# A sixth weight slot for the experts of a two-layer hybrid trunk, with the residual's place lent to it

## What is computed

```
for i in range(2):
    h = rms_norm(x) * (1 + sc1) + sh1
    x = x + g1 * mixer_i(h)                      # gdn_mixer, then fox_mixer
    h = rms_norm(x) * (1 + sc2) + sh2
    # 32 experts of (1024 x 512) gate-up and (256 x 1024) down weights, 2 of them for each token
    x = x + g2 * sum_k w_k * (silu(h @ gate_e) * (h @ up_e)) @ down_e
return rms_norm(x, final_norm)
```

## Time and profile before

| | |
|---|---|
| Three timed runs | 1463.05, 1465.35, 1469.11 us; median 1465.35 us |
| The profiled execution | 1467.78 us, of which the span of instructions is 1466.2 us |
| TensorE busy in the span | 1337.1 us (91%) |
| VectorE, ScalarE, GpSimd busy | 731.8, 435.3, 397.0 us |
| Mean granted TensorE clock | 0.96 of full speed |
| DMA | 350.27 MB, mean 239 GB/s |
| Expert stages, first gather issued to last down product | 537.3 to 789.1 us and 1182.6 to 1437.2 us |

### The profile page before, as it was taken

How to read it: one execution, slowest core, us unless ns; L and a number is a source line. 1 busy time by engine, 2 the same in 40 slices (tenths; PEclk the granted TensorE clock), 3 DMA queues, 4 the chain that set the end, 5 groups by cost and what they waited for, 6 DMA issues and landing times.

```text
span 1466.2 us, 24949 instructions
## 1 busy us (share of the span) xinstructions
PE 1337.1 (91%) x9111; PEld 859.8 (59%) x9111; DVE 731.8 (50%) x1520; ACT 435.3 (30%) x1033; POOL 397.0 (27%) x588
## 2 busy tenths in 40 slices
PE   4999999999999989999886999999999979999881
PEld 2677767777775455555442777777764545555440
DVE  3656566667652466522223445666654557322224
ACT  4434424434442110000002645555541200000002
POOL 3022022112230023444334054434410024344320
PEclk8899999999999989999898899999999999999996
DMA  8255554512154279999997222122046379999995
GB/s 360 115 208 201 215 213 177 197 59 115 58 222 131 114 263 405 418 418 419 421 420 319 90 88 73 73 80 108 26 191 239 154 277 415 421 419 418 419 398 200
DMA packets 56693, 350.27 MB, mean 239 GB/s; under 512 B 18408, under 2 KB 18880, under 8 KB 30992
## 3 DMA queue, kind: packets, MB, share of 16 engines
q1 hardware_dynamic: 44992, 332.02, 57.1%
q0 software_dynamic: 11520, 16.83, 3.1%
q10 hardware_dynamic: 80, 0.04, 0.0%
HBM read 342.45 MB, written 27.34 MB: 252 GB/s over the span
## 4 chain that ended last, share of the span: by engine, by line
PE 70%; DMA 15%; DVE 9%; issue 2%; ACT 2%; POOL 1%; SPq 0%; POOLq 0%; DVEq 0%; ACTq 0%
PE PS L1116 10%; PE PS L771 8%; DMA hT<-in_moe_w_down_dram 8%; PE PS L773 7%; PE PS L772 7%; PE PS L1059 6%; PE PS L1123 5%; DMA Dr<-in_ada_w_dram 4%; PE PS L749 2%; PE PS L1143 2%; PE PS L1133 2%; PE PS L862 2%; PE PS L908 2%; PE PS L1108 2%; PE PS L1294 2%
## 5 line engine op out<-in xcount | busy, mean ns | idle before, releaser
L771 PE MATMUL PS<-hHi,Whi 128*128 128x512 f32 x512 | 225.3, 440 | 2.5 <-DVE hLo L1789 2.4
L773 PE MATMUL PS<-hHi,Wlo 128*128 128x512 f32 x512 | 202.8, 396 | 0.0
L772 PE MATMUL PS<-hLo,Whi 128*128 128x512 f32 x512 | 202.0, 394 | 0.0
L1360 ACT COPY arena<-PS 128x512 f32<-128x512 f32 (+4 forms) x256 | 108.6, 440 | 281.9 <-PE PS L862 104.7
L1116 PE MATMUL PS<-Wr,arena 128*64 128x256 f32 x1408 | 165.4, 389 | 9.8 <-DVE arena L2195 9.8
L1583 ACT ACTIVATE arena<-PS 128x128 f32<-128x128 f32 x72 | 20.0, 278 | 464.9 <-PE PS L1116 369.0
L1116 PEld LDWEIGHTS PS<-Wr,arena 128*64 128x64 f32 x1408 | 101.5, 140 | 88.8 <-issue 29.0
L2477 POOL DMA_INDIRECT y_rows<-arena x72 | 77.0, 1070 | 258.5 <-DVE arena L2207 252.2
L2418 POOL TENSOR_TENSOR Wlo<-Wr,Whi (+1 forms) x72 | 94.0, 1324 | 178.7 <-ACT Whi L1360 178.7
L771 PEld LDWEIGHTS PS<-hHi,Whi 128*128 128x128 f32 x512 | 97.6, 191 | 33.8 <-issue 18.2
L2201 DVE TENSOR_TENSOR arena<-arena,PS 128x128 f32<-128x128 f32 x72 | 20.7, 288 | 185.6 <-ACT arena L1583 169.0
(11 more groups left out here) (394 smaller groups left out, 2301.6 us busy)
## 6 DMA issues: line engine op xcount, KB each, us to landing
Wr<-in_moe_w_gate_up_dram SPq DMA_DIRECT2D x52, 2048.0 KB
Dr<-in_ada_w_dram SPq DMA_DIRECT2D x42, 1024.0 KB, 26.8
Dr<-in_moe_w_down_dram SPq DMA_DIRECT2D x28, 1024.0 KB
arena<-in_moe_w_gate_up_dram SPq DMA_DIRECT2D x14, 2048.0 KB
hT<-in_moe_w_down_dram SPq DMA_DIRECT2D x26, 1024.0 KB
Wr<-in_gdn_w_dram SPq DMA_DIRECT2D x8, 2048.0 KB, 8.6
Wr<-in_fox_w_dram SPq DMA_DIRECT2D x8, 2048.0 KB, 8.1
shift_scale<-in_moe_w_down_dram SPq DMA_DIRECT2D x12, 1024.0 KB
```

The source lines that it names most:

```text
L771: mm(out_ap, a_hi, b_hi, start=(k == 0), stop=False)
L772: mm(out_ap, a_hi, b_lo, start=False, stop=False)
L773: return mm(out_ap, a_lo, b_hi, start=False, stop=(k == KD - 1))
L1360: return nc.scalar.copy(dst, src)
```

## The change

- `FIRST` and `SLOTS` go from 5 to 6. The plan keeps 36 items and 33 places; expert 5 becomes one with an item of its own, and one ranked item fewer is planned at the end.
- The sixth down slot is a new tensor `spare` of 2048 columns, in which the first mixer's masks and sums now lie. It is asked for early (`down_load(i, 5, 5)`, right behind the down loads of slots 0 and 1). `busy` multiplies by `before` in place of `negmask`.
- The sixth gate-up slot is `X`. The residual is stored to `x_rows` (2048 KB) when the first two gathers have landed, the sixth gate-up matrix is asked for when that store has landed, and the residual is read back (2048 KB) when the last item that uses the slot has its gate-up product. `combine` waits for that.
- The down loads of slots 2, 3 and 4 are asked for behind that store, and so after the first two gathers have landed, in place of at `r_ps`.

```diff
-FIRST = 5
-SLOTS = 5
+FIRST = 6
+SLOTS = 6
...
-        if n < g - 1:
+        if n < g - 2:
             rank_at.append(one)
...
+        spare = sb("spare", [P, 2048])
+        negmask = spare[:, 0:LEVELS * P].rearrange("p (l j) -> p l j", l=LEVELS)
...
-        down_w = [Dr[:, 0, :], Dr[:, 1, :], hT_rows[:, 0:2048], hT_rows[:, 2048:4096], shift_scale[:].rearrange("p s d -> p (s d)")]
+        down_w = [Dr[:, 0, :], Dr[:, 1, :], hT_rows[:, 0:2048], hT_rows[:, 2048:4096], shift_scale[:].rearrange("p s d -> p (s d)"), spare[:]]
         up_rows = [arena[:, 0:KD * T] if u is None else Wr[:, u].rearrange("p k n -> p (k n)") for u in (3, 1, None, 0, 2)]
+        up_rows.append(X[:].rearrange("p n d -> p (n d)"))
...
                 for e in range(2):
                     down_load(i, e, e)
+                if i == 0:
+                    for a in range(2):
+                        sp.wait_ge(ada_out[a], 16 * ADA_HEADS)
+                down_load(i, 5, 5)
...
                 sp.wait_ge(r_ps, i + 1)
-                down_load(i, 4, 4)
-                for e in range(2, 4):
+                for u in range(2):
+                    sp.wait_ge(m["xg"][u], 16 + 4 * B)
+                load(x_rows.rearrange("(n p) d -> p n d", p=P), X[:], x_out)
+                for e in range(2, 5):
                     down_load(i, e, e)
+                sp.wait_ge(x_out, 16 * NT * i + 16 * (i + 1))
+                expert_load(i, 5, 5)
...
+                sp.wait_ge(m["gu_ps"], B + max(ENDS[p] for p in range(5, NP, SLOTS)) + 1)
+                load(X[:], x_rows.rearrange("(n p) d -> p n d", p=P), x_in)
                 if i == 0:
                     for p in range(2):
-                        sp.wait_ge(m["gu_ps"], max(ENDS[q] for q in ((28, 29), (30, 31))[p]) + 1)
+                        sp.wait_ge(m["gu_ps"], max(ENDS[q] for q in ((27, 28), (30, 31))[p]) + 1)
                         section_loads(fox_w, p, p, mix_w[p])
...
-                    mm(PS[7][:], ident[:], negmask[:, 0:4, :].rearrange("p l j -> p (l j)"), start=True, stop=True)
+                    mm(PS[7][:], ident[:], before[:].unsqueeze(1).to_broadcast([P, NT, P]), start=True, stop=True)
...
+                dve.wait_ge(x_in, 16 * (2 * i + 3))
                 for n in range(NT):
                     dve.wait_ge(y_in[n], 32 * (i + 2))
```

More of the change, by code:

```diff
@@ L65, in expert_plan @@
     for n, b in enumerate(GROUPS):
-        at = FIRST + 4 * n
-        big, low, one = FIRST + b, FIRST + 2 * g - 1 + 2 * n, FIRST + g + n
+        at = len(rank_at)
+        big, low, one = FIRST + b, FIRST + 2 * g - 2 + 2 * n, FIRST + g + n
         rank_at += [big, low, low + 1]
@@ L185, in build @@
         halves_r = sb_over(halves_at, "halves_r", [P, P])
-        negmask = sb("negmask", [P, LEVELS, P])
-        negtri = sb("negtri", [P, P])
+        spare = sb("spare", [P, 2048])
+        negmask = spare[:, 0:LEVELS * P].rearrange("p (l j) -> p l j", l=LEVELS)
+        negtri = spare[:, LEVELS * P:KD * P]
+        ada_acc, ada_bias = (spare[:, a:a + 2 * ADA_W].rearrange("p (i c) -> p i c", i=2) for a in (KD * P, KD * P + 2 * ADA_W))
         rows_at = sb_next()
@@ L208, in build @@
         own = sb("own", [P, 1])
-        ada_acc = sb("ada_acc", [P, 2, ADA_W])
-        ada_bias = sb("ada_bias", [P, 2, ADA_W])
         modc = sb("modc", [P, 2, KD])
@@ L383, in build @@
         mix_w = sems("mix_w", 2)
[L384 to L387, removed]
+        moe_w = sems("moe_w", 4) + [ada_in[0], sem("moe_w5")]
+        moe_w_from = (0, 0, 0, 0, 16 * 6 * ADA_HEADS, 0)
+        moe_d = sems("moe_d", 2) + [small_in, small2_in, ada_in[1], first_rows_ok]
+        moe_d_from = (0, 0, 16 * 4, 16 * 6, 16 * 4 * ADA_HEADS, 2)
         n_rs, n_h, n_tr, n_ta, n_tb = sem("n_rs"), sem("n_h"), sem("n_tr"), sem("n_ta"), sem("n_tb")
@@ L516, in after_projection @@
                 else:
-                    sp.wait_ge(x_out, 16 * NT)
+                    sp.wait_ge(x_out, 16 * (NT + 1))
                     load(X[:], x_rows.rearrange("(n p) d -> p n d", p=P), x_in)
@@ L691, in _ @@
                 load(out[0, n * P:n * P + P, :], X[:, n, :], x_out)
-            sp.wait_ge(x_out, 2 * 16 * NT)
+            sp.wait_ge(x_out, 2 * 16 * (NT + 1))
         @block.tensor
@@ L1380, in h_parts @@
                 if phase:
-                    act.wait_ge(x_out, 16 * NT)
+                    act.wait_ge(x_out, 16 * (NT + 1))
                 act.wait_ge(n_tb, 4 * phase + NT)
@@ L1985, in out_projection @@
                 ins.then_inc(r_pos, 1)
-                dve.wait_ge(x_in, 16 * (layer + 2))
+                dve.wait_ge(x_in, 16 * (2 * layer + 2))
                 dve.wait_ge(gate_in, 48 * layer + 16)
```

## The result

The changed kernel took 1479.74 us (median of 8 runs, 1474.95 to 1484.41); the kernel before took 1469.63 us beside it (8 runs, 1463.05 to 1472.95). The ratio is 1.0076, 95% interval 1.0051 to 1.0101: slower, by 11 us (7 to 15). The forecast was slower with 0.75, at 1482 us in a range of 1466 to 1491. The profiled execution took 1479.44 us, its span is 1477.7 us.

The account below looks back on a forecast made before the run. The prediction took DMA bytes to bind the expert stages, with TensorE about level. Layer 0 +9.0, layer 1 +5.5, clock +2.0 and tail +0.5 made +17.0 us on 1465.35: 1482 us, range 1466 to 1491.

Parts of the forecast that it names:

- What binds: Expert stages: bytes bind, 417 GB/s at DMA share 1.01, TensorE about level; the only unused DMA time is the head gap.
- rival 4: Expert stages: TensorE sets the pace, the sixth slot removes the weight waits, 23.0 us, giving 1439 us; chance 0.10.
- rival 5: Sixth gate-up matrix lands after its item's turn, 34 us into the stage; at 10 us late, 1492 us; chance 0.03.
- The bytes and the earlier start: Each layer's stream: 4.2 MB more, 10.1 us; restart on the second gather, 5.4 us (layer 0) and 8.9 us (layer 1) sooner.
- Rival 2: Stage heads: gathers land as before, restarts win only 4.1 and 6.9 us; +3.3 us, 1486 us; chance 0.15.
- Where the last down matrix landed: Stage ends: last down matrix forecast to land at 791.9 us in layer 0 and 1436.5 us in layer 1.
- The order at the end: Stage ends: last gate-up matrix lands 2.5 us before the last byte, then the last item's whole 8.7 us chain follows.
- Bytes and TensorE end together: Layer 0's stage end, kernel before: last down matrix landed at about 787.2 us, just when its product began.
- Rival 3: Stage ends: last down matrix alone decides, 4.3 us off each layer and no clock term; +6.4 us, 1472 us; chance 0.17.
- The clock: Last item, behind a weight wait: slower TensorE clock costs +1.0 us in each layer, bounds 0 and 2.7.
- The tail: Behind layer 0's stage: residual's way back hidden before the first combine; later loads pushed back cost +0.5 us, bounds 0 and 5.
- The sum: Whole kernel: 9.0 + 5.5 + 2.0 + 0.5 = 17.0 us on 1465.35, so 1482 us.

Follow-up runs that it names:

- all of it early: Changed kernel with the residual's store ahead of the router's wait, one-item experts reordered, and down matrices 4, 2, 3 asked for at the router's product: 1464.12 us, ratio 0.9984.
- the held-back downs: Kernel before, five slots, with only the down loads of slots 2, 3 and 4 held until the first two gathers landed: 1465.57 us, ratio 0.9975.
- the other order: Changed kernel with one-item experts in all groups but the first and fourth, in place of all but the last two: 1477.63 us, ratio 1.0061.
- the side edits alone: Kernel before with only masks and sums in `spare` and `before` in place of `negmask` in the filler: 1466.20 us, ratio 0.9998.
- the lending alone: Changed kernel with down matrices 4, 2 and 3 asked for at the router's product, as before the change: 1472.66 us, ratio 1.0036.

## Why the prediction was right

**What binds.** Right. The rate in the plateau stayed at 417 to 419 GB/s and share 1.01 with a slot more, and 2.10 MB more or less behind the gathers moved the stage by 4.4 to 7.6 us, where 5.0 are worked out. The sixth slot (rival 4, 0.10) paid in no version: in the changed kernel the waits for weights grew by 6 to 7 us in each layer. With all of it early they are 10.1 and 8.0 us, fewer than before, but its stages, 274.2 and 271.1 us, are together no shorter than those of the held-back downs with five slots, 272.1 and 271.8. Fewer waits did not make a shorter stage. Nor was it late (rival 5): no wait for a matrix in `X` stands in the rows of the changed kernel.

**The bytes and the earlier start.** The 4.2 MB in each layer are there (8.4 on the page). The restart gain was put too low in layer 0: the restart stood 31.3 us behind the marker and now stands 23.5, so 7.8 us and not 5.4, beyond the bound of 6.6; in layer 1 34.1 and now 24.7, so 9.3 and not 8.9. What failed is the step that left layer 0's gather where it had landed, at 542.8, and took the filler's end for the bound. The filler bounds TensorE's turn; SyncE waits for the landing alone. Without down matrices ahead the first gather lands 3.1 to 3.7 us after its issue in either layer, 2 us sooner than the prediction left it, and the issue itself came 0.9 us sooner behind the marker. Rival 2 (the gathers don't gain, 0.15) falls with that, on the held-back downs alone and on these rows. The rule of the Trainium skill ("DMA: Bandwidth & Descriptors", section "Queues, rings and completion order") that the engines take turns between queues packet by packet is neither shown nor refuted by these runs, but it does not make a gather pass a backlog at no cost: that cost was 2 to 3 us behind 3.15 MB, and 3.5 behind 5.25.

**Where the last down matrix landed.** Take 5.0 us off the way back: 273.3 and 272.7 us behind the marker. The prediction's 791.9 and 1436.5 are 275.0 and 273.4 behind its markers, 1.7 and 0.7 later, of which most is the restart of layer 0.

**The order at the end.** Right on what the last item waits for, wrong on what the order is worth. TensorE's wait for the last gate-up matrix ended at 783.97 and 1437.72, and the way back landed at 791.4 and 1445.1: 7.4 us apart, which is the 3.15 MB of one down matrix and the residual. So the last gate-up matrix was 2.5 us ahead of the last down, and the chain behind it ran on to the end, 10.4 and 11.2 us. Counted from the markers, the last down matrix landed 3.0 and 0.5 us later than the 787.2 and 1435.3 of the prediction, and the stage ran 8.0 and 8.9 us beyond it in place of 1.9. So 6.0 and 6.9 us of the +9.0 and +7.4 are at the end; the prediction had 5.3 there (4.3 and 1.0 of clock).

But the late gate-up matrix as such is not what costs 4.3 us: with the order changed only 2.5 and 1.6 us came back, where the prediction's theory had 8 to 10 in all, since the wait moved up to the shared item's down matrix. "Bytes and TensorE end together" hid this. In the kernel before, the last product's matrix was there in time by that estimate, but TensorE's last wait for a weight ended 30.7 and 31.2 us before the end. In the changed kernel and with the other order a wait for some weight stands within 12.3 us of it. Rival 3 (the last down alone decides) is therefore out too: the stages end 8.0 and 8.9 us behind the last down matrix in the changed kernel, and 5.6 and 7.6 with the other order, not 1.94.

**The clock.** +1.0 in each layer was low: the last item's gate-up product took 5.34 and 6.14 us against 3.62, so 1.7 and 2.5. In layer 1 the granted clock around it, 1436 to 1440 us, was 0.50, the lower of its two levels (1.2 GHz); the wait of 4.24 us came before it (the window is shown in the last section).

**The tail.** Hidden, as put. The first combine began at 807.95, 13.5 us behind the stage's end; it was 13.6. The stretch from layer 0's end to layer 1's marker is 373.0 us, where it was 373.9.

**The sum.** The stages grew by 16.4 us by the profiles, against 16.5 worked out (9.0 + 5.5 + 2.0), because a restart gain put 2.8 us too low and a clock put 2.2 us too low nearly cancel, which is luck. So is part of the fit of the time itself. The change was forecast at +17 us; timed it is +11 (7 to 15), and 17 lies outside. That 1482 is only 2.3 us from 1479.74 comes from the start of the sum: 1465.35, from three runs, was 4.3 us under the median of eight. The profiled executions are only 11.7 apart, since the first stage of the changed one began 3.8 us earlier, and the timed medians 10.1. That the start is no effect of the change is likely and not proven: the side edits alone gave nothing, and the first markers of the seven kernels with the lending lie between 513.1 and 521.0 us, those of the three without it between 514.8 and 517.3. Against the mean of the two executions of like work the stages grew by 15.2 us, just above the interval of the timing (7.5 to 14.8); the 4 us between the two figures stay open.

## What to carry to other kernels

With the DMA engines' share at 1.0 in the stage, another buffer slot did not shorten it here. It cost the bytes that made room for it: in full where they stood in the stream, and nothing that could be measured where the store stood in the gap ahead of it. What a move into or out of a gap brings depends on what the restart waits for: the same three loads, held back, won 4 us where the loads behind them waited for a product, and cost 6 where they waited for the gathers. Ask where the last wait for data lies and how much work is behind it, and not only when the last byte lands. Count the stage from a marker of its own: it leaves out when the stage began, which moved by up to 8 us between executions, though two executions of like work still differed by 0.9 and 1.4 us.

## What the runs showed of the hardware that was not expected

A gather of 64 rows on its own queue took 3.1 to 3.7 us from issue to landing with no down matrix asked for ahead of it (nine stages in which TensorE waited for it, three of them with the 2.10 MB store of the residual ahead), 5.4 to 6.5 in five stages of six with the 3.15 MB of down matrices ahead (before, the side edits, the lending alone in layer 0), and 7.0 and 7.1 with 5.25 MB ahead. In the sixth, layer 1 of the lending alone, its issue came 1.9 us later behind the marker than before, and it took 3.8; that speaks for the backlog that is left, not what was asked for, but it is one stage. Whether the gather waits for it or shares the engines with it, no run here separates.

The end of the plateau is not sharp. The end of layer 1's stage in the changed kernel, in windows of 4 us (the last three columns are granted clock, DMA share and GB/s):

```profile
1428.00:1432.00 4.00, 4.00 (x63) 2.22 (x57) 0.69 (x3) 0.49 (x2) 1.18 (x2) 1.00 0.98 406
1432.00:1436.00 4.00, 1.49 (x8) 0.29 (x4) 1.04 (x2) 0.00 (x0) 0.92 (x1) 0.99 0.80 331
1436.00:1440.00 4.00, 2.28 (x12) 1.49 (x14) 0.00 (x0) 0.00 (x0) 0.24 (x2) 0.50 0.62 252
1440.00:1444.00 4.00, 4.00 (x25) 2.33 (x21) 0.00 (x0) 0.10 (x1) 0.00 (x0) 0.66 0.20 81
```

The queue is not empty before 1445.1 (the way back's landing), yet the share falls from 1432 us on. The kernel before shows the same in its layer 1: 0.76, 0.41 and 0.10 in the windows of 4 us from 1424 to 1436 us. The last gate-up matrix of the changed kernel came in the middle of the fall, at 1437.72. My reading is that some engines had run dry before others, and that the late matrices wait for those that lag; the share is a mean over the 16 engines, no view lists them one by one, and no experiment took it away.
